# Up pass of a mixed expert layer: two of three gathered token blocks summed on VectorE, one on TensorE

## The chip, the core and the metric

The kernel runs on one core of a Trainium2 chip. A core has TensorE (matrix products, PE in the profile), VectorE (DVE), ScalarE (ACT), GpSimd (POOL) and SyncE (SP), an on-chip memory of 128 partitions (SBUF), eight banks of accumulators (PSUM) that TensorE writes, and 16 DMA engines. The metric is the time of one execution on the device in microseconds.

## The reference, cut to what matters

The whole layer is a block of two sequence mixers and a feed-forward part, with 1024 tokens of width 1024. The change lies in the feed-forward part, in its last step. Each token has 8 heads x 16 = 128 picked experts out of 16384, with one row of `expert_up` each:

```
u = expert_down[idx]
act = gelu(einsum('thkd,td->thk', u, xb), approximate=False)
v = expert_up[idx]
return einsum('thk,thkd->td', (g * act).astype(xb.dtype), v)
```

Then the sum is normalised, scaled by a gate and added to the residual. All data is float32.

## The kernel before

The tokens are eight blocks of 128. The kernel computes the step in two ways at once. Five blocks (`ND`, the dense ones) take all 16384 experts as a dense product: the coefficient of every expert for every token (zero where it isn't picked) times `expert_up`. The other three (`NA = 3`, the gathered ones) fetch only the picked rows.

**The dense part** runs in 32 groups (`GROUPS`) of four chunks of 128 experts (`GT = 4`). For a chunk n, SyncE loads `up_raw`, `gelu_in` (`gu`) and `weights_in` (`w`), each with two buffers (lines 2176 to 2184). VectorE multiplies `gu` by `w` (L2341), ScalarE casts the product to its high part (L2277), VectorE subtracts it for the low part (L2343). ScalarE casts `up_raw` to `up_hi` (L2275) and GpSimd subtracts that for `up_lo` (`cut`, L2227). TensorE then does ten slots (`SLOTS`: five token blocks x two halves of 512 columns) for the group, each 12 matmuls (L2451) into one of five PSUM banks, and VectorE adds each finished slot to `y_acc` (L2353). Chunks of group g are prepared while TensorE works on group g - 1: ScalarE starts a group when all slots of group g - 2 are done (L2270), and TensorE when all four low parts of both kinds are there.

**The gathered part.** Before the change blocks 0 and 1 are TensorE's (`NP = 2`), and block 2 (`OWN`) is VectorE's.
- TensorE's blocks: GpSimd fetches for one token its 128 picked rows, one to a partition, 512 KB (L2210, `fetch`, ring `rows` of six). Four such fetches make a `quad` (line 2404): 8 matmuls of 32 columns of weights (16 instructions in the trace, L2413), in which the coefficients stand in a column of `spread` that VectorE makes (L2320). A block is 32 quads, two quads go to a group, before slot 1 and slot 6. The sums of a block gather in `ps_r` over all its quads, and ScalarE copies them out (`keep_rows`, L2265): for block 0 in the middle of the pass, in group 16, between two of its casts (lines 2278 to 2281), and TensorE waits for that before it begins block 1 (line 2407).
- VectorE's block: a fetch takes the c-th picked row of every token, token by partition (L2220, `fetch_own`, ring `own_rows` of two), and VectorE adds it, times a coefficient per partition, to `y_acc` (L2333, `add_own`). 128 adds, four to a group.

**Order.** All queues are in order and written out by hand. GpSimd's for a group (lines 2240 to 2253): cut 0, one own fetch, four fetches, cut 1, own fetch, cut 2, own fetch, four fetches, cut 3, own fetch. A fetch waits until its buffer's last reader is done: `fetch` for `quad_done`, `fetch_own` for `own_added`. VectorE's for a quarter j of group g (lines 2355 to 2365): product, wait for ScalarE, low part, one own add, then the slots of group g - 1, two or three of them; at the group's end the spreads. SyncE's for a chunk: `up_raw` once the cut two chunks back is done, `gelu_in` and `weights_in` once the low part two chunks back is done.

**The end.** VectorE does the last own adds, then takes the last ten slots and between them finishes the eight blocks (square sum on ScalarE, then three instructions each, L2370 to L2376) in the order `FINISH`.

## Time and profile before

| | us |
|---|---|
| median of 3 runs | 4108.4 (4105.47 to 4109.06) |
| the profiled execution | 4111.73 |
| its span, first to last instruction | 4110.0 |
| mean granted TensorE clock | 0.972 |
| busy: PE / DVE / ACT / POOL | 3846.8 / 2647.5 / 1692.5 / 1784.0 |
| up pass | from about 3036 to the end |
| DMA, whole span | 956.46 MB, mean 233 GB/s |

Engine names are those above; PEld is TensorE's load of weights. L2451 is line 2451 of the kernel before. In a row of a timeline, what stands in brackets is how long the engine was idle before the instruction, and what ended that. Matmuls overlap, so the time of one (some 0.39 us) is longer than the distance to the next.

### The profile page before, as it was taken

The page shows a single profiled execution, that of the slowest core. Times are in us where ns is not written, and L with a number is a line of the kernel's source. Part 1 is how long each engine was busy: PE and PEld are TensorE (multiplying, and loading weights), DVE is VectorE, ACT ScalarE, POOL GpSimd, SP SyncE. Part 2 cuts the span into 40 slices and gives each one's busy share as a digit, 9 for nine tenths or more (in the row PEclk, how much of TensorE's full clock was granted, in tenths as well). Part 3 has the DMA queues.
Part 4 walks back from the last instruction along what each step waited for, and adds up shares of the span by engine and source line. Part 5 has one row for each costly group of instructions (what it writes and reads, how often), then busy time and mean ns, then how long its engine had stood idle before and what let it go on. Part 6 is the DMA issues. An engine that isn't in the chain of part 4 may idle for free. (4 is left out here: it accounts for less than half of the span.)

```text
span 4110.0 us, 58100 instructions
## 1 busy us (share of the span) xinstructions
PE 3846.8 (94%) x21214; PEld 3214.6 (78%) x21214; DVE 2647.5 (64%) x4884; ACT 1692.5 (41%) x3247; POOL 1784.0 (43%) x1275
## 2 busy tenths in 40 slices
PE   8899999989899969978999999999969999999998
PEld 3688888856677769978999999999956777677776
DVE  3455411138775425689999989997756666666666
ACT  2123343358422431125777777777611222222222
POOL 0233333349544212123333233335447677676774
PEclk9999999999999989989999999999979999999999
DMA  8222233357566332167888888899999999999998
GB/s 308 53 78 97 97 102 100 103 180 253 180 183 200 103 128 61 49 226 242 255 265 273 262 276 272 268 286 351 359 308 339 347 352 347 334 341 350 343 345 295
DMA packets 639573, 956.46 MB, mean 233 GB/s; under 512 B 198996, under 2 KB 416740, under 8 KB 638436
## 3 DMA queue, kind: packets, MB, share of 16 engines
q1 hardware_dynamic: 319492, 423.09, 31.3%
q0 software_dynamic: 110592, 402.70, 28.1%
q10 hardware_dynamic: 209248, 127.55, 10.0%
q8 instruction: 140, 2.29, 0.2%
q14 instruction: 101, 0.83, 0.1%
HBM read 807.33 MB, written 145.88 MB: 232 GB/s over the span
## 5 line engine op out<-in xcount | busy, mean ns | idle before, releaser
L1909 POOL DMA_INDIRECT down_rows<-in_peer_down_dram,row_ids x384 | 451.3, 1175 | 856.7 <-DVE row_u L2049 769.7
L1930 PE MATMUL p_u<-h2T_hi,downT_hi 128*128 128x320 f32 x2048 | 656.8, 321 | 11.7 <-ACT gelu_out L1980 11.7
L1930 PE MATMUL p_u<-h2T_lo,downT_hi 128*128 128x320 f32 x2048 | 636.9, 311 | 0.0
L1930 PE MATMUL p_u<-h2T_hi,downT_lo 128*128 128x320 f32 x2048 | 636.0, 311 | 0.0
L2049 DVE CUSTOM_DVE_ANT_0 gate_rows<-down_rows,x_tok_rows 128x1024 f32<-128x1024 f32 x384 | 469.1, 1222 | 84.9 <-DMA down_rows<-in_peer_down_dram,row_ids 72.0
L2451 PE MATMUL p_y<-up_hi,coef_hi 128*128 128x512 f32 x1240 | 494.2, 399 | 19.3 <-DVE coef_lo L2343 9.2
L2451 PE MATMUL p_y<-up_lo,coef_hi 128*128 128x512 f32 x1240 | 486.5, 392 | 0.0
L2451 PE MATMUL p_y<-up_hi,coef_lo 128*128 128x512 f32 x1240 | 484.7, 391 | 0.0
L517 PE MATMUL p<-hT_hi,w_hi 128*128 128x512 f32 x1024 | 405.6, 396 | 0.0
L1930 PEld LDWEIGHTS p_u<-h2T_hi,downT_hi 128*128 128x128 f32 x2048 | 388.8, 190 | 13.9 <-issue 13.8
L517 PE MATMUL p<-hT_hi,w_lo 128*128 128x512 f32 x1024 | 399.3, 390 | 0.0
L517 PE MATMUL p<-hT_lo,w_hi 128*128 128x512 f32 x1024 | 399.1, 390 | 0.0
L1930 PEld LDWEIGHTS p_u<-h2T_lo,downT_hi 128*128 128x128 f32 x2048 | 388.6, 190 | 0.0
L1930 PEld LDWEIGHTS p_u<-h2T_hi,downT_lo 128*128 128x128 f32 x2048 | 387.6, 189 | 0.0
L2353 DVE TENSOR_TENSOR y_acc<-p_y,y_acc 128x512 f32<-128x512 f32 x310 | 212.2, 688 | 203.7 <-PE p_y L2451 203.2
L2227 POOL TENSOR_TENSOR up_lo<-up_raw,up_hi 128x1024 fp32r<-128x1024 f32 x128 | 322.0, 2516 | 27.3 <-ACT up_hi L2275 25.2
L2451 PEld LDWEIGHTS p_y<-up_hi,coef_hi 128*128 128x128 f32 x1240 | 233.8, 189 | 124.3 <-issue 64.2
L2210 POOL DMA_INDIRECT up_rows<-in_peer_up_dram,row_ids_turned x256 | 273.1, 1067 | 93.5 <-issue 77.1
L2277 ACT CAST coef_hi<-gelu_in 128x640 fp32r<-128x640 f32 x128 | 93.1, 728 | 481.1 <-DVE gelu_in L2341 481.1
L2451 PEld LDWEIGHTS p_y<-up_hi,coef_lo 128*128 128x128 f32 x1240 | 234.0, 189 | 50.6
L471 POOL CAST w_hi<-w_raw 128x1024 fp32r<-128x1024 f32 x64 | 66.5, 1039 | 472.5 <-issue 238.6
L2451 PEld LDWEIGHTS p_y<-up_lo,coef_hi 128*128 128x128 f32 x1240 | 234.1, 189 | 46.3
(355 smaller groups left out, 8105.1 us busy)
## 6 DMA issues: line engine op xcount, KB each, us to landing
down_raw<-in_peer_down_dram SPq DMA_DIRECT2D x128, 512.0 KB, 5.9
up_raw<-in_peer_up_dram SPq DMA_DIRECT2D x128, 512.0 KB, 5.8
scratch_gu<-gelu_out ACTq DMA_DIRECT2D x128, 320.0 KB, 5.4
gelu_in<-scratch_gu SPq DMA_DIRECT2D x128, 320.0 KB, 5.3
weights_in<-scratch_w SPq DMA_DIRECT2D x128, 320.0 KB, 6.9
w_raw<-in_w_in_dram SPq DMA_DIRECT2D x64, 512.0 KB, 3.9
w_ada_sb<-in_w_ada_dram SPq DMA_DIRECT2D x12, 2048.0 KB, 14.5
scratch_w<-weights_out ACTq DMA_DIRECT2D x40, 512.0 KB
```

The costliest lines, as they stand in the source:

```text
L471: pool.tensor_copy(w_hi[:, u], w_raw[:, u]).then_inc(hi_done, 1)
L517: mm = pe.matmul(ps[u][:, half, :], w[:, u, k, :], hT[h][:, k, half * TH:(half + 1) * TH], start=(n == 0), stop=(n == 3 * KD - 1))
L1909: pool.indirect_dma_start(out=rows[:, c % RING, :], out_offset=None, in_=inp["peer_down"][0], in_offset=bass.IndirectOffsetOnAxis(ap=row_i ...
L1930: mm = pe.matmul(ps_u[half][:, 0:HD], d[:, n % 3, k, :], h2[h][:, k, half * HD:(half + 1) * HD], start=(j == 0), stop=(j == 3 * KD - 1))
L2049: dve.tensor_tensor_reduce(junk, rows[:, c % RING, :], x_tok[:, a], 1.0, 0.0, ALU.mult, ALU.add, row_u[:, a, k:k + 1]).then_inc(dot_done, 1)
L2210: pool.indirect_dma_start(out=rows[:, r % RING, :], out_offset=None, in_=inp["peer_up"][0], in_offset=bass.IndirectOffsetOnAxis(ap=ids_t[: ...
L2227: pool.tensor_tensor(up_lo[:, g % 2, j, :], up_raw[:, u], up_hi[:, g % 2, j, :].bitcast(F32), ALU.subtract).then_inc(up_lo_done, 1)
L2277: act.copy(g_hi[:, v, j, :], gu[:, u]).then_inc(g_hi_done, 1)
L2353: dve.tensor_tensor(part, ps_y[s % BANKS][:], part, ALU.add).then_inc(added, 1)
L2451: mm = pe.matmul(ps_y[s % BANKS][:], a[:, v, j, t * P:(t + 1) * P], b[:, v, j, half * TH:(half + 1) * TH], start=(n == 0), stop=(n == 3 * ...
```

## The change

`NP` becomes 1: block 0 stays TensorE's, blocks 1 and 2 are VectorE's (`NO = 2`, 256 own fetches and adds, eight of each to a group, two to a quarter). `RING` goes from six to four, `RING_OWN` from two to four, so that the eight row buffers stay eight; `SPREADS` from four to two. A group has one quad, before slot 1; the first group one instead of two. GpSimd's order for a group is cut 0, two own fetches, four fetches, and then three times a cut and two own fetches. The copy of block 0's sums falls out of the middle of the pass and is done at the end. `FINISH` becomes blocks 1, 2, 3, 4, 5, 0, 6, 7. The ids of two blocks are now cast without a transpose.

```
-    NP = NA - 1
-    OWN = NA - 1
-    FINISH = (*range(NP - 1), OWN, *range(NA, TB - 2), NP - 1, TB - 2, TB - 1)
-    RING = 6
+    NP = NA - 2
+    NO = NA - NP
+    FINISH = (*range(NP - 1), *range(NP, NA), *range(NA, TB - 2), NP - 1, TB - 2, TB - 1)
+    RING = 4
     SPREADS = 2 * NP
-    RING_OWN = 2
+    RING_OWN = 4
...
                 def fetch_own(c):
+                    a, k = NP + c // P, c % P
                     if c == 0:
                         pool.wait_ge(own_ids, 1)
                     if c >= RING_OWN:
                         pool.wait_ge(own_added, c - RING_OWN + 1)
                     pool.indirect_dma_start(out=own_rows[:, c % RING_OWN, :], out_offset=None, in_=inp["peer_up"][0],
-                                            in_offset=bass.IndirectOffsetOnAxis(ap=ids_t[:, OWN, c:c + 1], axis=0)
+                                            in_offset=bass.IndirectOffsetOnAxis(ap=ids_t[:, a, k:k + 1], axis=0)
                                             ).then_inc(own_loaded[c % RING_OWN], 16)
...
-                for r in range(4):
+                for r in range(RING):
                     fetch(r)
                 fetch_own(0)
+                fetch_own(1)
                 cut(0, 2)
                 cut(0, 3)
-                for r in range(4, RING):
-                    fetch(r)
-                fetch_own(1)
+                fetch_own(2)
+                fetch_own(3)
                 for g in range(1, GROUPS):
-                    r, c = (g - 1) * 4 * NP + RING, (g - 1) * GT + RING_OWN
-                    cut(g, 0)
-                    fetch_own(c)
-                    for i in range(4):
-                        fetch(r + i)
-                    cut(g, 1)
-                    fetch_own(c + 1)
-                    cut(g, 2)
-                    fetch_own(c + 2)
-                    for i in range(4, 8):
-                        fetch(r + i)
-                    cut(g, 3)
-                    fetch_own(c + 3)
+                    c = (g - 1) * GT * NO + RING_OWN
+                    for j in range(GT):
+                        cut(g, j)
+                        for i in range(NO):
+                            fetch_own(c + j * NO + i)
+                        if j == 0:
+                            for i in range(4):
+                                fetch(4 * g + i)
...
-                    elif t == OWN:
-                        act.wait_ge(own_added, P)
+                    elif t < NA:
+                        act.wait_ge(own_added, P * (t - NP + 1))
...
                 def add_own(c):
                     dve.wait_ge(own_loaded[c % RING_OWN], 16 * (c // RING_OWN + 1))
-                    if c == 0:
-                        dve.tensor_scalar(acc[:, OWN, :], own_rows[:, 0, :], coef[:, OWN, 0:1], None, ALU.mult
+                    a, k = NP + c // P, c % P
+                    if c:
+                        dve.wait_ge(own_added, c)
+                    if k == 0:
+                        dve.tensor_scalar(acc[:, a, :], own_rows[:, c % RING_OWN, :], coef[:, a, 0:1], None, ALU.mult
                                           ).then_inc(own_added, 1)
                         return
-                    dve.wait_ge(own_added, c)
-                    dve.scalar_tensor_tensor(acc[:, OWN, :], own_rows[:, c % RING_OWN, :], coef[:, OWN, c:c + 1],
-                                             acc[:, OWN, :], ALU.mult, ALU.add).then_inc(own_added, 1)
+                    dve.scalar_tensor_tensor(acc[:, a, :], own_rows[:, c % RING_OWN, :], coef[:, a, k:k + 1],
+                                             acc[:, a, :], ALU.mult, ALU.add).then_inc(own_added, 1)
...
                         if g:
-                            add_own((g - 1) * GT + j)
+                            for i in range(NO):
+                                add_own(((g - 1) * GT + j) * NO + i)
...
-                for j in range(GT):
-                    add_own((GROUPS - 1) * GT + j)
+                for i in range(GT * NO):
+                    add_own((GROUPS - 1) * GT * NO + i)
...
-                            elif j % 2:
-                                quad(j // 2)
+                            elif j == 1:
+                                quad(0)
```

## Rows read from the trace of the kernel before

**Rows 1.** The page's part 4: the chain that ended last, by line:
```profile
PE p_y L2451 20%; PE p_rows L2413 3%; DMA weights_in<-scratch_w 0%; POOL up_rows L2210 0%; DVE gelu_in L2341 0%; DVE y_acc L2372 0%; POOL up_lo L2227 0%; DVE y_acc L2353 0%; DMA up_own_rows<-in_peer_up_dram,row_ids_turned 0%; PE p_y L2432 0%; DMA up_raw<-scratch_x 0%; DVE y_acc L2376 0%; ACT coef_hi L2277 0%; DVE y_acc L2350 0%; POOL up_own_rows L2220 0%
```

**Rows 2.** The chain in order of time: start us, us, what:
```profile
3126.67 13.87 PE p_y L2451 x60
...
3567.43 1.85 PE p_rows L2413 x16
3569.28 11.15 PE p_y L2451 x48
3580.43 4.56 issue
3584.99 5.21 PE p_y L2451 x12
...
4066.10 1.90 PE p_rows L2413 x16
```

**Rows 3.** Windows: us, busy us of each engine, PEclk, DMA share, GB/s:
```profile
2800.00:2900.00 100.00, 100.00 (x738) 99.94 (x737) 74.43 (x113) 71.53 (x174) 51.19 (x43) 1.00 1.03 361
...
3300.00:3450.00 150.00, 150.00 (x726) 110.88 (x719) 103.24 (x115) 33.51 (x38) 104.29 (x78) 1.00 0.97 351
```

**Rows 4.** Who waited for whom, from 2480 us on: us, times, longest:
```profile
DVE y_acc L2353 <- PE p_y L2451: 203.2, 163, 4.1
```

**Rows 5.** Own adds: ns min/median/max, first and last start:
```profile
L2333 DVE SCALAR_TENSOR_TENSOR y_acc<-up_own_rows,row_coef,y_acc x127: 1272/1279/1298, 3073.5 to 4077.6; 128x1024 f32<-128x1024 f32 x127
```

**Rows 6.** VectorE's timeline: start us, us, line, [idle before <- releaser]:
```profile
3312.38 2.99 DVE L2341 TENSOR_TENSOR gelu_in<-gelu_in,weights_in 128x640 f32<-128x640 f32 x1
3316.16 0.83 DVE L2343 TENSOR_TENSOR coef_lo<-gelu_in,coef_hi 128x640 fp32r<-128x640 f32 x1 [0.79 <-ACT coef_hi L2277]
...
3319.94 0.82 DVE L2341 TENSOR_TENSOR gelu_in<-gelu_in,weights_in 128x640 f32<-128x640 f32 x1
...
3324.78 0.69 DVE L2353 TENSOR_TENSOR y_acc<-p_y,y_acc 128x512 f32<-128x512 f32 x1 [0.59 <-PE p_y L2451]
3327.50 0.69 DVE L2353 TENSOR_TENSOR y_acc<-p_y,y_acc 128x512 f32<-128x512 f32 x1 [2.03 <-PE p_y L2451]
...
3328.50 0.82 DVE L2341 TENSOR_TENSOR gelu_in<-gelu_in,weights_in 128x640 f32<-128x640 f32 x1
3330.12 2.13 DVE L2343 TENSOR_TENSOR coef_lo<-gelu_in,coef_hi 128x640 fp32r<-128x640 f32 x1 [0.79 <-ACT coef_hi L2277]
3332.18 1.27 DVE L2333 SCALAR_TENSOR_TENSOR y_acc<-up_own_rows,row_coef,y_acc 128x1024 f32<-128x1024 f32 x1
```

**Rows 7.** GpSimd's timeline over the same group:
```profile
3308.73 2.41 POOL L2227 TENSOR_TENSOR up_lo<-up_raw,up_hi 128x1024 fp32r<-128x1024 f32 x1
...
3312.27 2.41 POOL L2227 TENSOR_TENSOR up_lo<-up_raw,up_hi 128x1024 fp32r<-128x1024 f32 x1
...
3333.72 0.96 POOL L2220 DMA_INDIRECT up_own_rows<-in_peer_up_dram,row_ids_turned  x1 [2.15 <-DVE y_acc L2333]
3334.98 0.94 POOL L2210 DMA_INDIRECT up_rows<-in_peer_up_dram,row_ids_turned  x1 [0.30 <-issue]
...
3340.17 2.40 POOL L2227 TENSOR_TENSOR up_lo<-up_raw,up_hi 128x1024 fp32r<-128x1024 f32 x1
```

**Rows 8.** The page's part 6: KB each, median us to landing:
```profile
weights_in<-scratch_w SPq DMA_DIRECT2D x128, 320.0 KB, 6.9
```

**Rows 9.** Timelines of VectorE and GpSimd where the two meet:
```profile
3180.82 1.28 DVE L2333 SCALAR_TENSOR_TENSOR y_acc<-up_own_rows,row_coef,y_acc 128x1024 f32<-128x1024 f32 x1
...
3181.72 2.63 POOL L2227 TENSOR_TENSOR up_lo<-up_raw,up_hi 128x1024 fp32r<-128x1024 f32 x1
...
3757.39 1.28 DVE L2333 SCALAR_TENSOR_TENSOR y_acc<-up_own_rows,row_coef,y_acc 128x1024 f32<-128x1024 f32 x1
...
3757.48 2.00 POOL L2210 DMA_INDIRECT up_rows<-in_peer_up_dram,row_ids_turned  x1 [0.30 <-issue]
```

**Rows 10.** VectorE's timeline near the end: the last own add:
```profile
4077.60 1.28 DVE L2333 SCALAR_TENSOR_TENSOR y_acc<-up_own_rows,row_coef,y_acc 128x1024 f32<-128x1024 f32 x1 [0.19 <-DMA up_own_rows<-in_peer_up_dram,row_ids_turned]
```

More of the change, by code:

```diff
@@ L2231, in _ @@
                 cut(0, 1)
-                for r in range(4):
+                for r in range(RING):
                     fetch(r)
                 fetch_own(0)
+                fetch_own(1)
                 cut(0, 2)
                 cut(0, 3)
-                for r in range(4, RING):
-                    fetch(r)
-                fetch_own(1)
+                fetch_own(2)
+                fetch_own(3)
                 for g in range(1, GROUPS):
-                    r, c = (g - 1) * 4 * NP + RING, (g - 1) * GT + RING_OWN
-                    cut(g, 0)
-                    fetch_own(c)
-                    for i in range(4):
-                        fetch(r + i)
-                    cut(g, 1)
-                    fetch_own(c + 1)
-                    cut(g, 2)
-                    fetch_own(c + 2)
-                    for i in range(4, 8):
-                        fetch(r + i)
-                    cut(g, 3)
-                    fetch_own(c + 3)
-                for r in range((GROUPS - 1) * 4 * NP + RING, 4 * QUADS * NP):
-                    fetch(r)
-                for c in range((GROUPS - 1) * GT + RING_OWN, P):
+                    c = (g - 1) * GT * NO + RING_OWN
[6 more added lines that the diff above has]
+                                fetch(4 * g + i)
+                for c in range((GROUPS - 1) * GT * NO + RING_OWN, P * NO):
                     fetch_own(c)
@@ L2303, in _ @@
                 dve.tensor_copy(ids_t[:, 0:NP], ps_r[:, 0, 0:NP * P].rearrange("p (a t) -> p a t", t=P)).then_inc(ids_ready, 1)
-                dve.tensor_copy(ids_t[:, OWN], row_f[:, OWN]).then_inc(own_ids, 1)
+                dve.tensor_copy(ids_t[:, NP:], row_f[:, NP:]).then_inc(own_ids, 1)
                 dve.tensor_scalar(one_at[:], iota[:, 0:2 * QUADS], float(QUADS - 1), None, ALU.is_equal).then_inc(one_at_ready, 1)
```

## The prediction

> **What bounds the kernel now.** I read the page's chain of what ended last, then the chain in order of time, then windows and groups, and last the timelines of VectorE and GpSimd over one group of the up pass. The page's chain puts 20% of the span on the dense matmuls of line 2451 and 3% on the quads of line 2413, next to nothing on anything else [rows 1]: in the up pass TensorE is the bound. The chain in time shows the beat: 1.85 us for a quad, 13.87 us for five slots, again and again [rows 2]. A group (ten slots, two quads) is 2 x 15.72 = 31.44 us, and there are 31 after the first. In a steady 150 us TensorE is busy all the time at clock 1.00 (2.4 GHz); VectorE is at 103.24 (69%), GpSimd at 104.29, and the DMA engines move 351 GB/s [rows 3]. VectorE's slack is real but split: it waits for finished slots 203.2 us in all, 6.55 us a group [rows 4], in pieces such as 0.59 and 2.03 us [rows 6]. One loss stands apart: where TensorE goes from block 0 to block 1 of the gathered rows, the chain shows 4.56 us of issue and 5.21 us for 12 matmuls that elsewhere take 2.72 (13.87 - 11.15) [rows 2], 7.05 us in all. There ScalarE copies the finished sums out (line 2281) ahead of its casts.
>
> **TensorE's part.** One quad of two goes from each group. Two halves of 60 matmuls without one are 2 x 60 x 0.227 (2.72 / 12) = 27.2 us; with one quad (1.85, and the 0.27 by which five slots behind one exceed 5 x 2.72) the group is 29.3 us, 2.1 less than now. It is a gain only if everything else can also finish a group in 29.3 us. The switch of blocks goes, with its 7.05 us.
>
> **VectorE's part.** Four more adds of own rows a group, 4 x 1.28 = 5.1 us [rows 5], and one spread fewer (0.2). VectorE now uses 31.44 - 6.55 = 24.9 us of a group, waits for ScalarE and collisions counted in; with the change 29.8 us. That alone would take all but 1.6 of the 2.1 us back: 1.6 us a group would be left.
>
> **GpSimd's part.** The number of fetches is the same (12 a group), but their order isn't. A fetch of own rows waits for the add that frees its buffer, and everything behind it on GpSimd's queue waits too: the fetches for TensorE's block, and the next cut (line 2227). With a ring of four and two adds for each quarter of a group, the fetches behind cut j wait for the two adds of the same quarter j (own_added at least c - 3, with c = 2j + 4 and 2j + 5 counted from the group's first). So cut j + 1 can't begin before both adds are done. SyncE loads the next up_raw once a cut is done, and gelu_in and weights_in stand behind that load in its queue (lines 2179 to 2184): what waits for the cut is VectorE's product of line 2341 two quarters on.
>
> **The chain through it.** I follow it from the second cut of one group to that of the next, 3308.73 to 3340.17, which is 31.44 us [rows 7]. Cut (2.41), loads, product at 3319.94 (8.80 us after the cut's end; a load of weights_in lands 6.9 us from issue [rows 8], and two issues go ahead, so some 7.9 is needed and 0.9 is slack), the quarter's add, waits for TensorE of 0.59 and 2.03 us [rows 6], product at 3328.50, the lower part, which takes 2.13 us instead of 0.83 because a cut runs (1.30 more), the add at 3332.18 [rows 6], own fetch at 3333.72, four fetches 1.26 us and more apart, next cut [rows 7]. Without its slack (0.9 + 0.59 + 2.03 = 3.5) the chain is 27.9 us. The change lays on it two adds (one in the last quarter, one in the first; 2.56 us) and one own fetch ahead of the four (1.26): 31.8 us, before any new collision. It takes the place of TensorE as the bound.
>
> **New collisions.** The two engines stop each other. A cut that began 0.90 us after an own add took 2.63 us instead of 2.41, and ended 2.25 us behind the add; a fetch that began 0.09 us after an own add (3757.39 and 3757.48) took 2.00 us instead of 0.94, to 0.81 us behind the add's end; the product at 3312.38 took 2.99 us instead of 0.82 behind the cut at 3312.27 [rows 5 to 7, 9]. No own add is in the trace that began during a cut (they take 1.27 to 1.30 us throughout); the reverse case and the lower part behind a cut let me take one as able to lose up to 2.4 us. Now look at the order of the new quarter: add, add, with the fetch released by the first coming 0.27 us behind its end, inside the second. It ends 0.81 us behind the second add, and the second fetch starts some 0.85 us later than it could: 0.85 us on the chain once. And a cut, which now lands 1.3 to 2 us behind the second add, meets the next product or its lower part nearly every time, since only two or three adds from PSUM (0.69 each) lie between. On the chain are the last quarter, in which nothing collides today, and the first: between 0 and a whole cut (2.4 us) more. I take 0.6, nearer to none, since the first quarter's loss of 1.30 is counted already. Period: 31.8 + 0.85 + 0.6 = 33.2 us; bounds 31.8 (nothing new) and 35.9 (a cut's full length, a second 0.85 among TensorE's four fetches).
>
> The Trainium skill ("SBUF - State Buffer", Who interferes with whom) has one port pair as an exclusive lock: VectorE instructions with two SBUF inputs contend with GpSimd instructions that read SBUF, and the loser blocks until the other is done. The trace agrees for cut and product, and shows the fetch blocked too.
>
> **Start, tail.** The first group and the start change by about one add more (1.3 us). In the tail VectorE adds eight own rows instead of four before the last ten slots are taken. Today the last one starts at 4077.60, having waited for its rows [rows 10], 14.2 us behind the last group's start (its first quad is at 4066.10, one slot of 2.72 in [rows 2]), and VectorE's finishing of the blocks runs on from there. With eight, the last four rows can be asked for only as the first four are added: 4.8 us to the first add, about 1.3 and 1.2 us to the fetches, some 6 us to landing, in two rounds: 17 to 18 us, 2.9 us later. Bounds 0 and 6. TensorE's block has one copy at the end, as now. The smaller transposes and casts at the start are worth nothing that shows.
>
> **A wait that is added to TensorE.** The one quad of a group wants the spread that VectorE makes at the end of its group. If TensorE starts the group as soon as the last lower part is there, the quad comes 2.7 us later, the spread 4.5 to 7. TensorE then waits up to 4.4 us. It costs nothing in the forecast, since TensorE has 33.2 - 29.3 = 3.9 us to spare and starts a little later in the next group.
>
> **The sum.** 30 periods from the first full group to the last, each 33.2 - 31.44 = 1.76 us longer: +52.8. Switch of blocks: -7.05. Start +1.3, tail +2.9. Together +50. The profiled execution took 4111.7 us (span 4110.0, 1.7 around it): 4161.7 with the change. The median of the runs is 3.3 below the profiled one: **4158 us**.
>
> **Rivals.**
> 1. TensorE stays the bound at 29.3 us. For it: the averages, as both other engines have over 30% idle. Against it: VectorE alone needs 29.8 and the chain 31.8. 30 x -2.1 = -63; -7 + 4.2; 4042 us. At VectorE's 29.8: 30 x -1.64 = -49, 4056 us. Together 13%.
> 2. The slack on the chain is larger than I read (own fetches find buffers free, since VectorE runs ahead), and the period lies between 29.9 and 31.3: 4060 to 4100. 9%.
> 3. DMA becomes the bound. A group moves 351 GB/s x 31.44 us = 11.0 MB. The fastest 100 us in the trace, in the pass before, had 361 GB/s [rows 3]: 30.6 us a group, 30 x -0.84 - 2.8 = -28, 4080 us. Against: the rate was set by demand there. 5%. The Trainium skill ("SBUF - State Buffer", A bandwidth-pool intuition that's wrong) gives about 358 GB/s from HBM to a core; an estimate by it is 30.8 us a group and 4087 us, and the trace already shows a little more.
> 4. The added work just replaces the removed: period 31.3 to 31.7, within 0.2% of before (4100 to 4117). 10%.
> 5. The forecast, 31.8 to 34.7 us: 4119 to 4203. 50%.
> 6. Worse: each own add that meets a cut is held for it, and the late cuts delay the loads again; 34.7 to 36.5 us: 4203 to 4257. 13%.
>
> The forecast ends slower; rivals 1 to 3 end faster, and the point is a period of 31.3 us: below it the change gains. A measurement of this kernel can tell about 0.2% (8 us) from no change. Faster 0.27, same 0.10, slower 0.63. The range leaves out rival 1 and the upper half of the worst case, and takes in the rest: 4065 to 4230.
>
> **What would show it.** Right: in the steady groups the dense matmuls stop every group for some 4 us waiting for a lower part or a spread; quads come 32 to 35 us apart; line 2353 hardly waits for TensorE any more (203 us to under 40); the products, lower parts and own adds have longer means, own adds some of 2 us and more; fetches of line 2220 often 2.0 us; VectorE's share over 75%; DMA rate falls to about 330 GB/s; the stall at the switch is gone. Wrong: quads 29.3 to 31.3 us apart with TensorE without a gap. If own adds stay at 1.28 us although cuts run beside them, the upper bound falls. If weights_in is waited for in each group, the loads and not the adds carry the chain.

## The result and the profile after

The changed kernel takes 4234.7 us (median of four runs, 4225.3 to 4241.6), the one before 4107.0 in the same session (four runs); the ratio is 1.0309, with a 95% interval of 1.0285 to 1.0333. It is slower, as forecast, but by 128 us where +50 was forecast, 4.7 us above the upper end of the range. The profiled execution took 4230.0 us (span 4228.2), 118.3 more than that of before.

I time the groups by GpSimd's first cut in each, and call the time from one to the next the period. From group 2 to group 31 (29 periods) the mean was 31.95 us before (TensorE's own beat of 31.44 us in about half of the groups, longer in the others, with the stall at the switch of blocks) and is 36.13 us now: 29 x 4.17 = +121 us. All that lies around these periods is 2.7 us shorter. So one number is to be explained: a period of 36.1 us, where 33.2 was forecast.

Part 4 of the profile's page (share of the span by what stands on the chain) showed TensorE and next to nothing else before [rows 1]. Now it reads:
```profile
DVE 8%; POOL 6%; issue 5%; DMA 5%; PE 3%; ACT 1%; SPq 0%; DVEq 0%; POOLq 0%
```
TensorE has gone from 23% to 3%; VectorE, GpSimd, loads and the hand-overs between them carry the up pass. The same 150 us as in [rows 3], and within it one stretch in which TensorE starts on a quad after a wait (columns as there; the second answer is of TensorE alone):
```profile
3300.00:3450.00 150.00, 131.38 (x574) 98.26 (x573) 123.45 (x113) 28.71 (x33) 107.85 (x67) 0.95 0.88 307
...
3462.80:3466.50 3.70, 3.67 (x17) 0.50 0.73 204
```
VectorE is up from 103.24 to 123.45 us of 150, the DMA engines are down from 351 to 307 GB/s. Who waited for whom in the up pass (us in all, times, longest):
```profile
POOL up_own_rows L2221 <- DVE y_acc L2329: 233.6, 72, 4.0
...
PE p_rows L2410 <- DVE row_spread L2314: 120.7, 31, 4.2
...
DVE y_acc L2349 <- PE p_y L2448: 78.5, 59, 2.3
...
DVE gelu_in L2337 <- DMA weights_in<-scratch_w: 29.7, 21, 8.6
```
TensorE now waits in each of the 31 groups for the spread, 3.9 us; VectorE's wait for TensorE [rows 4] has fallen from 203.2 to 78.5 us.

VectorE's groups of instructions in the up pass (busy us, mean ns of one, idle before), first of before, then of after:
```profile
L2341 DVE TENSOR_TENSOR gelu_in<-gelu_in,weights_in 128x640 f32<-128x640 f32 x128 | 172.3, 1346 | 22.4 <-DMA weights_in<-scratch_w 21.8
...
L2343 DVE TENSOR_TENSOR coef_lo<-gelu_in,coef_hi 128x640 fp32r<-128x640 f32 x128 | 149.7, 1170 | 106.6 <-ACT coef_hi L2277 106.6
L2320 DVE TENSOR_TENSOR row_spread<-row_coef_turned,row_one_at 128x128 f32<-128x128 f32 x64 | 19.9, 353 | 0.0
```
```profile
L2329 DVE SCALAR_TENSOR_TENSOR y_acc<-up_own_rows,row_coef,y_acc 128x1024 f32<-128x1024 f32 x254 | 364.5, 1435 | 17.2 <-DMA up_own_rows<-in_peer_up_dram,row_ids_turned 4.0
...
L2339 DVE TENSOR_TENSOR coef_lo<-gelu_in,coef_hi 128x640 fp32r<-128x640 f32 x127 | 159.2, 1253 | 100.8 <-ACT coef_hi L2271 100.8
L2337 DVE TENSOR_TENSOR gelu_in<-gelu_in,weights_in 128x640 f32<-128x640 f32 x126 | 144.7, 1148 | 29.7 <-DMA weights_in<-scratch_w 29.7
L2314 DVE TENSOR_TENSOR row_spread<-row_coef_turned,row_one_at 128x128 f32<-128x128 f32 x32 | 87.1, 2723 | 0.0
```
Own adds are up from 1.28 [rows 5] to 1.44 us in the mean, lower parts from 1.17 to 1.25, the spread from 0.35 to 2.72; products are down from 1.35 to 1.15. One group in VectorE's timeline (start us, us, idle before and releaser):
```profile
3444.16 4.63 DVE L2329 SCALAR_TENSOR_TENSOR y_acc<-up_own_rows,row_coef,y_acc 128x1024 f32<-128x1024 f32 x2
...
3450.47 3.51 DVE L2337 TENSOR_TENSOR gelu_in<-gelu_in,weights_in 128x640 f32<-128x640 f32 x1 [0.48 <-DMA weights_in<-scratch_w]
...
3455.51 2.67 DVE L2329 SCALAR_TENSOR_TENSOR y_acc<-up_own_rows,row_coef,y_acc 128x1024 f32<-128x1024 f32 x2
...
3459.89 2.89 DVE L2314 TENSOR_TENSOR row_spread<-row_coef_turned,row_one_at 128x128 f32<-128x128 f32 x1
3462.70 0.81 DVE L2337 TENSOR_TENSOR gelu_in<-gelu_in,weights_in 128x640 f32<-128x640 f32 x1
...
3465.05 2.67 DVE L2329 SCALAR_TENSOR_TENSOR y_acc<-up_own_rows,row_coef,y_acc 128x1024 f32<-128x1024 f32 x2
```
and in GpSimd's:
```profile
3445.07 2.63 POOL L2228 TENSOR_TENSOR up_lo<-up_raw,up_hi 128x1024 fp32r<-128x1024 f32 x1
...
3450.88 2.40 POOL L2228 TENSOR_TENSOR up_lo<-up_raw,up_hi 128x1024 fp32r<-128x1024 f32 x1
3457.06 1.95 POOL L2221 DMA_INDIRECT up_own_rows<-in_peer_up_dram,row_ids_turned  x1 [3.77 <-DVE y_acc L2329]
3459.31 0.94 POOL L2221 DMA_INDIRECT up_own_rows<-in_peer_up_dram,row_ids_turned  x1 [0.30 <-issue]
3460.27 2.35 POOL L2228 TENSOR_TENSOR up_lo<-up_raw,up_hi 128x1024 fp32r<-128x1024 f32 x1
3466.59 1.95 POOL L2221 DMA_INDIRECT up_own_rows<-in_peer_up_dram,row_ids_turned  x1 [3.98 <-DVE y_acc L2329]
3468.85 0.94 POOL L2221 DMA_INDIRECT up_own_rows<-in_peer_up_dram,row_ids_turned  x1 [0.30 <-issue]
...
3475.55 2.78 POOL L2228 TENSOR_TENSOR up_lo<-up_raw,up_hi 128x1024 fp32r<-128x1024 f32 x1
```
Read them side by side. The product at 3450.47 (0.82 us when undisturbed) takes 3.51 and the spread at 3459.89 (0.28) takes 2.89: by the records each began 0.4 us ahead of a cut and ended 0.7 and 0.2 us behind its end (3450.88 to 3453.28, 3460.27 to 3462.62), which is a cut's length too late. Two own adds take 2.67 us; the pair at 3444.16 took 4.63, with a whole cut in it (3445.07). Own fetches that start inside the second add of a pair (3457.06, 3466.59) take 1.95 us instead of 0.94. This holds for the whole up pass of the changed kernel: 96 of VectorE's products, lower parts, own adds and spreads take over 0.1 us more than their usual time. Every one of them overlaps a cut and ends 0.16 to 1.09 us behind the end of it, and not one that meets no cut is longer than usual. And the order closes on itself: the pair of adds releases two own fetches, the cut comes right behind them, and that is where VectorE stands at its next product or spread.

### The profile page after: what moved, and what is told of

Read it like the earlier page. It is cut to its first block and busy times, and to the rows that moved or that the text cites. A ratio compares the mean times of both kernels' runs of the same rounds, so it can differ in the third digit from the quotient of the medians.

```text
span 4228.2 us, 57230 instructions
## 1 busy us (share of the span) xinstructions
PE 3833.0 (91%) x20700; PEld 3212.5 (76%) x20700; DVE 2893.2 (68%) x4980; ACT 1688.1 (40%) x3246; POOL 1888.5 (45%) x1275
## 3 DMA queue, kind: packets, MB, share of 16 engines
q0 software_dynamic: 110592, 402.70, 27.9%
## 5 line engine op out<-in xcount | busy, mean ns | idle before, releaser
L1909 POOL DMA_INDIRECT down_rows<-in_peer_down_dram,row_ids x384 | 460.2, 1198 | 843.7 <-DVE row_u L2049 754.5
L2221 POOL DMA_INDIRECT up_own_rows<-in_peer_up_dram,row_ids_turned x256 | 353.8, 1382 | 288.5 <-DVE y_acc L2329 233.6
L2329 DVE SCALAR_TENSOR_TENSOR y_acc<-up_own_rows,row_coef,y_acc 128x1024 f32<-128x1024 f32 x254 | 364.5, 1435 | 17.2 <-DMA up_own_rows<-in_peer_up_dram,row_ids_turned 4.0
```

The source lines that it names most:

```text
L1909: pool.indirect_dma_start(out=rows[:, c % RING, :], out_offset=None, in_=inp["peer_down"][0], in_offset=bass.IndirectOffsetOnAxis(ap=row_i ...
L2221: pool.indirect_dma_start(out=own_rows[:, c % RING_OWN, :], out_offset=None, in_=inp["peer_up"][0], in_offset=bass.IndirectOffsetOnAxis(ap ...
L2329: dve.scalar_tensor_tensor(acc[:, a, :], own_rows[:, c % RING_OWN, :], coef[:, a, k:k + 1], acc[:, a, :], ALU.mult, ALU.add).then_inc(own_ ...
```

## The experiments

The main theory: **the cut on GpSimd and VectorE's instructions with two operands in SBUF exclude each other, and VectorE's chain pays for it at whatever stands beside the cut** (theory A in the expectations). The rivals: the late spread and TensorE's stall (B); the order of GpSimd's queue (own fetches waiting for adds, everything behind them waiting too), whatever the port does (C); VectorE's time as such, since it has four adds more (D), or that time with a fixed loss for each cut wherever it stands (E); the loads or the DMA rate.

Three runs were timed once only: half of the added adding, the memset cut in the changed kernel, and the doubled adds with the cut on GpSimd. The others are medians of two to eight executions, which lie at most 18 us apart.

**The spread is made earlier.** In the changed kernel, ahead of the group's last product instead of behind its last add:
```diff
                     for j in range(GT):
+                        if j == GT - 1:
+                            spread_rows(g)
                         coefs(g, j)
...
-                    for q in range(NP):
-                        spread_rows(g * NP + q)
```


> The changed kernel with one edit: VectorE makes the spread of a group before its fourth product, not behind its last adds. In the changed kernel a steady group takes 36.35 us; TensorE waits 120.7 us in all for the spread, and its quad, coming behind that wait, takes 3.64 us instead of 1.85. Theory A (the chain cut, loads, product, adds, fetches, cut sets the period, lengthened by the port that VectorE and GpSimd share): the cut that now holds the spread up will hold the next product up instead, so the chain loses little: period 34.5 to 36.3 us, 4175 to 4230 us, while TensorE's wait for the spread is gone. Theory B (TensorE, held up behind the spread and slow afterwards, sets the period together with VectorE): it loses 4 + 1.8 us a group and the period falls to 32 us or less, 4100 us or less.


Measured: 4223.7 us, ratio 1.0283 (1.0242 to 1.0325), period 35.7 us, as theory A had it. The spread takes 0.33 us now and TensorE doesn't wait for it at all. But the cut is still paid for, now by the product:
```profile
L2337 DVE TENSOR_TENSOR gelu_in<-gelu_in,weights_in 128x640 f32<-128x640 f32 x128 | 316.4, 2472 | 32.6 <-DMA weights_in<-scratch_w 32.1
...
L2314 DVE TENSOR_TENSOR row_spread<-row_coef_turned,row_one_at 128x128 f32<-128x128 f32 x32 | 10.6, 330 | 0.0
```
Products went from 1.15 to 2.47 us in the mean, and TensorE waits for the lower part instead (134.2 us in all). The stall of TensorE is a consequence, not the cause.

**Half of the added adding.** The first add of each pair covers 8 of its 1024 columns, so most of half the own sums is left out:
```diff
-                    dve.scalar_tensor_tensor(acc[:, a, :], own_rows[:, c % RING_OWN, :], coef[:, a, k:k + 1],
-                                             acc[:, a, :], ALU.mult, ALU.add).then_inc(own_added, 1)
+                    n = D if c % 2 else 8
+                    dve.scalar_tensor_tensor(acc[:, a, :n], own_rows[:, c % RING_OWN, :n], coef[:, a, k:k + 1],
+                                             acc[:, a, :n], ALU.mult, ALU.add).then_inc(own_added, 1)
```


> The changed kernel with the first add of each pair of own rows cut to 8 of 1024 columns (that part of the sums of blocks 1 and 2 is left out); all fetches, waits and their order stay. Theory A: two such adds lie on the chain (1.2 us each), and the cut that stands beside them changes place: 33 to 34.5 us a group, 4120 to 4175 us. If only the order on GpSimd's queue and the number of own fetches counted (theory C), it stays at 4215 to 4235. If VectorE's total time alone set the period (theory D), it falls by all four adds, 4.8 us a group, to TensorE's pace behind the spread: 4080 to 4100.


Measured: 4189.6 us, period 34.4. Four adds a group, 0.22 us each instead of 1.28, are 4.2 us less work for VectorE, and they gave back 1.7 us a group. Lower parts and spread stayed as dear as in the changed kernel (1.26 and 2.72 us), and products and the full adds became dearer (1.37 and 1.57 us, after 1.15 and 1.44). This is outside all three forecasts, and says that the arithmetic of the added adds is less than half of the loss.

**A cut that reads nothing.** In the changed kernel GpSimd fills the buffer three times instead of subtracting; the lower part of up_raw is left out of the sums:
```diff
-                    pool.tensor_tensor(up_lo[:, g % 2, j, :], up_raw[:, u], up_hi[:, g % 2, j, :].bitcast(F32),
-                                       ALU.subtract).then_inc(up_lo_done, 1)
+                    pool.memset(low, 0.0).then_inc(blank, 1)
...
+                    pool.memset(low, 0.0).then_inc(blank, 1)
...
+                    pool.memset(low[:, 0:TH], 0.0).then_inc(up_lo_done, 1)
```


> The changed kernel with each cut replaced by three memsets of up_lo on GpSimd (1024, 1024 and 512 columns, about 2.4 us together, as long as the cut; the low part of up is zero, so its share of the dense product is left out). GpSimd is busy as long and its queue is the same, but it reads nothing from on-chip memory. Theory A with the port as the mechanism: the product (3.5 us instead of 0.82) and the spread (2.89 instead of 0.28) are no longer held up, 5.3 us a group: 31 to 32.5 us, 4050 to 4110 us. If GpSimd's time and the order of its queue are the cause and not the port: 4210 to 4235 us.


Measured: 4104.6 us, 130 us less, period 31.9. GpSimd is as long at it (0.97 + 0.95 + 0.53 us and two hand-overs) and everything else is in its place, but VectorE is undisturbed:
```profile
L2334 DVE SCALAR_TENSOR_TENSOR y_acc<-up_own_rows,row_coef,y_acc 128x1024 f32<-128x1024 f32 x254 | 325.6, 1282 | 16.8 <-DMA up_own_rows<-in_peer_up_dram,row_ids_turned 3.5
...
L2342 DVE TENSOR_TENSOR gelu_in<-gelu_in,weights_in 128x640 f32<-128x640 f32 x128 | 106.2, 830 | 171.6 <-DMA weights_in<-scratch_w 171.6
L2344 DVE TENSOR_TENSOR coef_lo<-gelu_in,coef_hi 128x640 fp32r<-128x640 f32 x128 | 105.6, 825 | 101.6 <-ACT coef_hi L2276 101.6
...
L2319 DVE TENSOR_TENSOR row_spread<-row_coef_turned,row_one_at 128x128 f32<-128x128 f32 x32 | 8.9, 279 | 0.0
```
It is in the main theory's range. Of the 4.7 us by which a steady group had grown (36.1 - 31.44), 4.2 go with the exclusion. VectorE's account of the two runs agrees: from the memset run to the changed kernel its instructions take 212 us more, it waits 142 less for weights_in (171.6 us with memsets, 29.7 in the changed kernel) and 54 more for TensorE (24.2 and 78.5), which makes +124, where the spans differ by 125.3 us.

The run also gives a scale. With these four means as what an instruction costs alone, the excess of each kernel over them, by its own groups, is what its VectorE lost:

| kernel | cuts on GpSimd | VectorE lost, us | per cut, us | period, us |
|---|---|---|---|---|
| before | 128 | 114 | 0.9 | 31.95 |
| after | 128 | 212 | 1.7 | 36.1 |
| spread earlier | 128 | 281 | 2.2 | 35.7 |
| half of the added adding | 128 | 240 | 1.9 | 34.4 |
| four fetches apart (below) | 128 | 275 | 2.1 | 36.4 |
| own fetches later (below) | 128 | 213 | 1.7 | 34.4 |

(After, for one: 126 x (1.148 - 0.830) + 127 x (1.253 - 0.825) + 254 x (1.435 - 1.282) + 32 x (2.723 - 0.279) = 212 us, the brackets being means in us.) A cut is 2.4 us long; before, VectorE lost less than half of it, now it loses most. The period doesn't follow this column from kernel to kernel (281 us with 35.7, 212 with 36.1): it tells what VectorE's instructions lose, not how much of that the chain feels.

**The old kernel with its own adds doubled.** Each own add of the kernel before is made twice, so that block 2's sums come out twofold. No fetch, quad or ring is changed:
```diff
...
+                    dve.scalar_tensor_tensor(acc[:, OWN, :], own_rows[:, c % RING_OWN, :], coef[:, OWN, c:c + 1],
+                                             acc[:, OWN, :], ALU.mult, ALU.add).then_inc(own_added, 1)
+                    dve.wait_ge(own_added, 2 * c)
```


> The kernel before with each own add done twice (block 2's sums come out twofold), nothing else changed: same fetches, same quads. It gives VectorE the added work of the change alone. By averages VectorE would need 30.0 us of a group's 31.44 and nothing changes: 4105 to 4112. Theory A: the chain gets two adds (2.56 us) on its 27.9 and loses its slack, and the fetch released by the second add no longer falls inside another add: 31.4 to 33 us a group, 4107 to 4160 us.


Measured: 4170.9 us, 64 above before and 11 above the upper end of what the main theory gave, period 33.9; TensorE now stands in each group (busy 141.07 of 150 us). By averages nothing was to change, with VectorE at 69% before. And an own add can be held up:
```profile
3419.80 1.28 DVE L2333 SCALAR_TENSOR_TENSOR y_acc<-up_own_rows,row_coef,y_acc 128x1024 f32<-128x1024 f32 x1
3421.11 3.30 DVE L2336 SCALAR_TENSOR_TENSOR y_acc<-up_own_rows,row_coef,y_acc 128x1024 f32<-128x1024 f32 x1
...
3420.70 2.63 POOL L2227 TENSOR_TENSOR up_lo<-up_raw,up_hi 128x1024 fp32r<-128x1024 f32 x1
```
The second add began 0.41 us behind the cut's start, took 3.30 instead of 1.28 us, and ended 1.08 behind the cut's end.

**Other orders of GpSimd's queue.** In the changed kernel, once with TensorE's four fetches spread over three quarters instead of all in the first, once with the own fetches a quarter later, so that they find their adds done:
```diff
-                        if j == 0:
-                            for i in range(4):
-                                fetch(4 * g + i)
+                        for i in (0, 1) if j == 0 else (j + 1,) if j < 3 else ():
+                            fetch(4 * g + i)
```


> The changed kernel with GpSimd's four fetches for TensorE's block no longer all behind cut 0: two stand behind cut 0, one behind cut 1, one behind cut 2. In the changed kernel the way from cut 0 to cut 1 is 15.5 us of a 36.1 us group. Theory A, in the form that the runs so far leave (the chain through GpSimd's queue and the loads gives about 32 us a group, port collisions the other 4): the piece of the chain from cut 0 to cut 1 loses two fetches, 2.5 us, and the pieces behind it gain them where there is slack; but the cuts then meet other instructions of VectorE: 34 to 36 us a group, 4165 to 4228. Rival E (each cut costs VectorE the same stretch wherever it stands, so VectorE's own sum is the bound): no change, 4220 to 4240.


```diff
-                            fetch_own(c + j * NO + i)
+                            if c + (j - 1) * NO + i >= RING_OWN:
+                                fetch_own(c + (j - 1) * NO + i)
```


> The changed kernel with each pair of own fetches moved one cut later on GpSimd's queue, so that behind cut j stand the fetches whose buffers were freed in quarter j - 1; GpSimd no longer waits for the adds of the running quarter before the next cut (205 us of waiting in the changed kernel). The rows have one quarter less to land (about 9 us between issue and use against 6.0 to landing). Theory A: the waits for the adds leave the chain, a cut is then bound by its loads and by the cast of up_hi; 3 to 6 us a group less if the cuts don't collide more: 33 to 35 us, 4130 to 4200. Rival E (VectorE's sum with its stretches is the bound): the cuts come earlier, into the own adds, and the time stays at 4210 to 4250.


Measured: 4239.1 us (ratio 1.0333, 1.0300 to 1.0365), period 36.4, for the first, no gain, as rival E had it and not theory A: lower parts now take 1.95 us in the mean, products 0.90. For the second 4191.0 us (1.0215, 1.0180 to 1.0251), period 34.4, in theory A's range. GpSimd's wait for own adds falls from 234 to 34 us (102 us of waiting for TensorE's quads come in), and the cut lands on the adds:
```profile
L2330 DVE SCALAR_TENSOR_TENSOR y_acc<-up_own_rows,row_coef,y_acc 128x1024 f32<-128x1024 f32 x254 | 445.1, 1752 | 46.8 <-DMA up_own_rows<-in_peer_up_dram,row_ids_turned 34.2
```
So the queue's order is worth some 44 us, a third of the loss, but none of these orders gets below before, and the loss per cut doesn't fall (2.1 us in the first, 1.7 in the second).

**The cut is moved to VectorE.** In both kernels, between product and lower part, with all its readers as they were; GpSimd only issues fetches:
```diff
-                def cut(g, j):
-                    n, u = g * GT + j, j % 2
-                    pool.wait_ge(up_hi_done, n + 1)
-                    pool.tensor_tensor(up_lo[:, g % 2, j, :], up_raw[:, u], up_hi[:, g % 2, j, :].bitcast(F32),
-                                       ALU.subtract).then_inc(up_lo_done, 1)
...
+                    dve.wait_ge(up_hi_done, n + 1)
+                    dve.tensor_tensor(up_lo[:, v, j, :], up_raw[:, u], up_hi[:, v, j, :].bitcast(F32),
+                                      ALU.subtract).then_inc(up_lo_done, 1)
```
The changed kernel with it:


> The changed kernel with the cut moved from GpSimd to VectorE, between product and low part, where VectorE waits 0.79 us for ScalarE; GpSimd only issues fetches. VectorE does four instructions of about 1.2 us more a group, of which 0.8 each lie in that wait, and nothing on GpSimd holds the port but for moments. Theory A with the port: VectorE's sum is 25.7 + 4 x 0.45 = 27.5 us, below TensorE's 29.3; what is left is TensorE or the loads, 29.5 to 31.9 us a group: 4035 to 4105 us, faster than the changed kernel by 3% and perhaps than the kernel before. If not the port but the number of VectorE's instructions were the cause, it would be at 4228 or above.


The kernel before with it:


> The kernel before with the same move of the cut to VectorE, two blocks still on TensorE. TensorE's 31.44 us a group bounds it: 31.4 to 31.6 us, 4085 to 4107 us (its mean is 31.95 today, with the switch of blocks in it). Theory A says it gains little, since the collisions of the kernel before lie in slack.


The kernel before with it and with its own adds doubled:


> The kernel before with each cut moved to VectorE and each add of own rows made twice (block 2's sums come out twofold): the same four adds more a group that cost +64 us with the cuts on GpSimd. If the price of the added adds was paid to the port that VectorE shares with GpSimd's cuts, it is near nothing here: VectorE computed at about 24.9 + 5.1 us, less the time it lost to cuts, stays within TensorE's 31.5 us, time 4083 to 4097. Rival: the adds cost because VectorE's own time runs out; with four cuts of 1.2 us in addition VectorE would be later still, and the time 4140 to 4200.


Measured: 4019.4 us for the changed kernel, below what was expected (ratio to before 0.9800, 0.9780 to 0.9819); 4087.5 for the kernel before (0.9962, 0.9951 to 0.9973), 4094.8 with adds doubled (0.9983, 0.9971 to 0.9994). The changed kernel with its cuts on VectorE beats both. Its chain in time, in the form of [rows 2], and its window:
```profile
3211.54 1.85 PE p_rows L2402 x16
3213.39 27.47 PE p_y L2440 x120
3240.86 1.85 PE p_rows L2402 x16
...
3150.00:3300.00 150.00, 150.00 (x701) 116.65 (x703) 138.47 (x162) 36.74 (x43) 78.27 (x61) 1.00 1.00 381
3300.00:3450.00 150.00, 150.00 (x705) 116.20 (x696) 137.39 (x159) 34.34 (x41) 77.49 (x61) 1.00 0.99 376
```
The period is 29.3 us in nearly every group, TensorE's own, without a gap. The cut takes 1.22 us here; on GpSimd each cost VectorE 1.7 and GpSimd 2.4. The doubled adds, +64 us before, cost 7 us here, with the same four adds and four cuts more on VectorE: its time as such isn't the cause. The two runs without the exclusion differ too: with memsets the period was 31.9 us, with the cut on VectorE 29.3. These 2.6 us go with GpSimd's time for the cut and its hand-overs, which stand in its queue whatever the port does. The move to VectorE takes both away at once; the memset run parts them.

**Half of the cuts.** In the changed kernel those of odd chunks on VectorE, the others on GpSimd:
```diff
                 def cut(g, j):
                     n, u = g * GT + j, j % 2
+                    if j % 2:
+                        return
...
+                    if j % 2:
+                        dve.wait_ge(up_hi_done, n + 1)
...
+                        dve.tensor_tensor(up_lo[:, v, j, :], up_raw[:, u], up_hi[:, v, j, :].bitcast(F32),
+                                          ALU.subtract).then_inc(up_lo_done, 1)
```


> The changed kernel with the cuts of odd chunks on VectorE and those of even chunks left on GpSimd. All four on GpSimd gave a period of 36.1 us and 4235 us, all four on VectorE 29.3 us and 4019 us. If each cut on GpSimd costs VectorE's chain by itself, half of them give about half: period 32 to 34 us, 4100 to 4160. Rival: one of the four cuts carries the loss (the one of the quarter with the last product and the spread); then the time lies near one of the two ends, under 4070 or above 4190.


Measured: 4163.7 us, ratio 1.0153 (1.0124 to 1.0183), period 34.0. Four, two and no cuts on GpSimd give 36.1, 34.0 and 29.3 us. 4163.7 is just above the forecast; the loss per cut that is left is 2.5 us, since both now meet products or the spread.

**TensorE's relief alone.** In the kernel before, the quads of odd number aren't multiplied (blocks 0 and 1 lack half their sums); fetches, spreads and adds stay. Then the same with the three memsets in place of the cut:
```diff
+                    if n % 2:
+                        pe.nop().then_inc(quad_done, 1)
+                        return
```


> The kernel before, of which the quads with odd number are left out (their gathered rows are fetched and spread but not multiplied, so blocks 0 and 1 lack half their sums): the change's relief of TensorE alone, without the added adds. TensorE's computed group is 29.3 us (two halves of 60 matmuls, 1.85 for the quad), VectorE keeps its 24.9 us. If the relief is worth what the prediction said, the period is 29.3 to 30 us and the time 4040 to 4065. Rival: the chain over cut, load, product, add and fetch carries the kernel just behind TensorE already (computed at 27.9 us without slack, but with collisions unseen it could be 30 to 31), then 4070 to 4100.

> The kernel before without the quads of odd number (as in the run with one quad a group), and each cut on GpSimd replaced by three memsets of about the same length, so that the lower part of up_raw is left out of the sums and GpSimd's work beside VectorE reads nothing. With the real cuts this gave a period of 30.8 us with TensorE waiting each group for the fourth cut, at 360 GB/s of DMA. If collisions at the port held the chain there, it falls back to TensorE's 29.3 us (29.3 to 29.7, time 4030 to 4052) and the DMA rate rises to some 375 GB/s. Rival: the DMA engines (share 0.98, 360 GB/s) held it; then the period stays at 30.6 to 31 us and the time at 4065 to 4085.


Measured: 4078.1 us (ratio 0.9949, 0.9926 to 0.9971), period 30.95 (30.8 in most groups), and with memsets 4037.9 (0.9821, 0.9787 to 0.9855), period 29.7 at 373 to 375 GB/s. The first is the rival's result, the second is in the range of the port. Chain and GpSimd's timeline of the first, at the border of a group:
```profile
3316.08 1.17 issue
3317.25 2.98 PE p_y L2454 x12
3320.23 1.85 PE p_rows L2416 x16
...
3314.75 2.39 POOL L2227 TENSOR_TENSOR up_lo<-up_raw,up_hi 128x1024 fp32r<-128x1024 f32 x1
```
TensorE starts the group 0.11 us behind the end of the fourth cut (3317.14), having stood for 1.17 us; in the next group the cut ends at 3348.46 and TensorE goes on at 3348.56. So the kernel before had a second bound 0.6 us behind the first. Of the 1.65 us by which the mean period is above TensorE's 29.3, 1.3 go once the cut reads nothing; the DMA rate, 354 to 360 GB/s there, wasn't it.

## Why the prediction was right in direction and wrong in size

- **TensorE's part: right.** 29.3 us a group was computed, and it is what the kernel does with the cuts on VectorE (1.85 + 27.47). The stall at the switch of blocks is gone, as said.
- **VectorE's part: right as a count.** In the changed kernel with its cuts on VectorE it is busy (138.47 + 137.39) / 300 x 29.3 = 26.9 us a group, four cuts of 1.22 included.
- **The chain without new collisions: right, in part by luck.** 31.8 was computed; 31.9 is what the memset run shows. But the sum had 1.3 us of an old collision in it, which is absent there, and the memset run also has the held-up own fetch (0.85). Without the first and with the second the sum's own figure for that run is 31.8 - 1.3 + 0.85 = 31.35, so 0.55 us a group was missing, part of it the memsets' length (some 2.6 us with hand-overs, cut 2.4).
- **New collisions: the term that failed.** The sum had 1.3 (old) + 0.6 (new) = 1.9 us a group for cuts beside VectorE; 36.1 - 31.9 = 4.2 were lost. The step was "I take 0.6, nearer to none, since the first quarter's loss of 1.30 is counted already." In the group read above the product lost 2.69 and the spread 2.61 us, one of them with each of two cuts in a row, 5.3 us where 0.6 was added. These 2.3 (4.2 - 1.9) and the 0.55 above are the 2.9 us by which the period was short (36.1 - 33.2): 29 x 2.93 = +85 us. Against it stand 7 us at start and tail (below), and 8 us because the groups of before held 29 x (31.95 - 31.44) = 15 us over the steady period, not the 7 of the switch alone; with one period fewer in this count (2 us) that is the 68 us between +50 and +118.
- **Behind it stood a wrong reading of slack.** I took the chain of before, 31.44 long, and took 3.5 us of waits out to get 27.9. But a wait is also where a cut costs nothing. With less work for TensorE and none added the chain didn't fall to 27.9 but stopped at 30.8. VectorE's loss per group was 114 / 32 = 3.6 us before and 212 / 32 = 6.6 after: 3 us more, about as much as the period was short. The trace of before had shown how near the chain was. Beside the stall at the switch TensorE stood seven more times between 3120 and 4060 us, 4.0 us in all. One of these stops in the chain, and GpSimd's fourth cut of that group:
```profile
3169.26 0.72 issue
3169.97 3.00 PE p_y L2451 x12
...
3167.49 2.39 POOL L2227 TENSOR_TENSOR up_lo<-up_raw,up_hi 128x1024 fp32r<-128x1024 f32 x1
```
TensorE went on 0.09 us behind the end of that cut (3169.88), as it does in the groups read of the run with one quad. The 150 us of [rows 3] happen to hold no such stop.
- **The upper bound was nearly right.** 35.9, a cut's full length and a second 0.85, was given as the worst; the mean is 36.1. Its row (the product at 3312.38, held for 2.17 us [rows 6]) was in view, and "nearer to none" was chosen although the prediction itself said that a cut would meet a product or lower part "nearly every time". Rival 6 (34.7 to 36.5 us, 4203 to 4257) is what happened, and had 13%; the range took in only its lower half. The mechanism in it, own adds held for cuts, is seen (up to 3.25 us) but is the smaller part: 254 x 0.153 = 39 of 212 us, against 78 for the spread.
- **The late spread costs nothing: right.** Up to 4.4 us a group were forecast, 3.9 came, and taking them away moved the time by only 11 us (0.3%), which the intervals of the two ratios don't tell from nothing.
- **Start +1.3, tail +2.9: together wrong by 7 us,** -2.7 instead of +4.2. Own adds at the end span 4182.65 to 4197.1, 14.5 us, as the four of before did (4064.43 to 4078.9): fetches land while the first four are added.
- **What would show it:** TensorE's stop of some 4 us in each group, longer lower parts and adds, own fetches of 2.0 us, VectorE over 75% (82%), no stall at the switch: all seen. Not seen: products were to have a longer mean and went from 1.35 to 1.15 us, and VectorE's wait for TensorE was to fall under 40 us and fell to 78.5. DMA at "about 330 GB/s" was 307, fitting the longer period. Quads were to come 32 to 35 us apart and came 36.1.
- **Two slips in the arithmetic, without weight.** By the sum's own terms (-7.05 + 1.3 + 2.9 over 30 periods) the change gains below a period of 31.5 us, not 31.3, and a period of 31.8 gives 4116 us, not 4119.
- **DMA as a bound (rival 3): refuted.** 376 to 381 GB/s stood for 300 us, where 361 was taken as the best.

What stays open: how the 4.2 us divide between the chain's places when all four cuts are there, since a cut moved from one place only turned up at another; how much of the 4.2 us of adding that was left out went back to longer products and full adds, and how much to waits; and why VectorE is held for the cut even where its record begins first. A faster order that keeps the cuts on GpSimd wasn't found, which doesn't show that there is none.

## What to carry to other kernels

Where two engines exclude each other, price a collision by up to the whole length of the other engine's instruction at every place where it can land on the chain, and never take out a wait as slack before asking which collision it hides. A change that relieves the bounding engine should be tried together with the move that frees the next one: here the same change costs 3.1% with the cut on GpSimd and, with the cut on VectorE in both kernels, takes the time from 4087.5 to 4019.4 us. A cheap test of such a port is to replace the suspect with an equally long instruction that reads nothing.

## What the runs showed of the hardware

- A GpSimd subtraction (two operands of 128x1024, 2.4 us) and VectorE's instructions with two SBUF operands exclude each other: in the rows above the product takes 3.51 us for 0.82, an own add 3.30 for 1.28, the spread 2.89 for 0.28. By the records it isn't always the first to start that goes first: of the 96 held instructions of the changed kernel 58 start up to 0.6 us ahead of the cut. Slot adds, which take one operand from PSUM, have means of 0.68 to 0.69 us in every kernel. GpSimd memsets of the same buffer disturb nothing. The Trainium skill ("SBUF - State Buffer", Who interferes with whom) says that two-input VectorE instructions contend with GpSimd instructions that read SBUF, not with those that only write it; the memset run agrees, with VectorE's means at 0.83 and 1.28 us.
- I hadn't expected how regular the hold on fetches is: in the changed kernel a fetch that starts within such a VectorE instruction and is held ends 0.81 to 0.86 us behind that instruction's end. It takes up to 2.00 instead of 0.94 us beside an own add (1.95 at 3466.59) and 1.34 beside the product below. A fetch that starts within a slot add, with one operand in PSUM, takes 0.93 to 0.94 us. The Trainium skill ("SBUF - State Buffer", Who interferes with whom) infers that a tensor_tensor doesn't hold back descriptor generation. These rows of the changed kernel, VectorE's and then GpSimd's, speak against it:
```profile
3471.05 0.82 DVE L2337 TENSOR_TENSOR gelu_in<-gelu_in,weights_in 128x640 f32<-128x640 f32 x1
...
3470.09 0.94 POOL L2210 DMA_INDIRECT up_rows<-in_peer_up_dram,row_ids_turned  x1 [0.30 <-issue]
3471.34 1.34 POOL L2210 DMA_INDIRECT up_rows<-in_peer_up_dram,row_ids_turned  x1 [0.30 <-issue]
```
The product is a tensor_tensor that ends at 3471.87; the fetch ends at 3472.68, where the one before it, which began 0.96 us ahead of the product, took 0.94 us. It isn't one case: all 49 fetches that start within a lower part (a tensor_tensor too) take 1.18 to 1.32 us.
- One core moved 376 to 381 GB/s over 300 us. The Trainium skill ("SBUF - State Buffer", A bandwidth-pool intuition that's wrong) has some 358 GB/s from HBM to a core; the measurement decides. By an estimate from that figure of the Trainium skill a group (11.0 MB) takes 30.8 us, where 29.3 was measured.
- In the group read above TensorE ran the quad, after its wait of some 4 us for the spread, at a granted clock of 0.50 of 2.4 GHz (1.2 GHz), 3.64 us instead of 1.85. The 48 matmuls behind it took 12.11 us instead of the 11.15 of [rows 2]. Behind equal waits in other groups the quad took 2.6 to 3.6 us. It cost little here: with the spread made earlier these waits are gone, and the time falls by only 11 us.
